# Sharing one weight stream between pairs of token tiles, and loading ahead across block boundaries

## Chip, cores and metric

The kernel runs on one core of a Trainium2 chip (trn2). The metric is the device time of one execution in microseconds. Engines are named as in the profile: PE (TensorE; PEld is its weight load), DVE (VectorE), ACT (ScalarE), POOL (GpSimd, which issues the gathers) and SP (SyncE, which issues most other transfers).

## What is computed

One layer of a decoder, in float32, for a prompt of 1024 tokens and for 8 sample tokens that each continue a cached sequence. Cut to what matters here:

```python
def layer(x, c, core, lw):
    sh1, sc1, gt1, sh2, sc2, gt2 = adaln(c, w_ada, b_ada)
    h = rmsnorm(x, g_norm1) * (1 + sc1) + sh1
    rq, rk, rv, rg, aq, ak, av = mixer_projections(h, w_in, g_qn, g_kn)   # w_in: 1024 x 3584
    o_ret, o_att, state = core(rq, rk, rv, aq, ak, av)                    # retention + dilated attention
    x = x + gt1 * mixer_output(o_ret, rg, o_att, g_ret, w_out)            # w_out: 1024 x 1024
    h2 = rmsnorm(x, g_norm2) * (1 + sc2) + sh2
    x = x + gt2 * peer(h2, w_pq, sub_keys, peer_u, peer_v)                # w_pq: 1024 x 1024
```

`peer` scores 2 x 128 keys per token and head, keeps 16 experts of 16384, and for each of the 8 x 16 chosen experts reads one row of `peer_u` and one of `peer_v` (8 KB together, stored side by side as `uv`): a dot product with h2, a GELU times a softmax gate, and a weighted sum of the `peer_v` rows.

## The kernel before, in words

`build` runs three blocks, one after the other. `condition` computes the six tables of the conditioning vectors from w_ada, in 12 chunks of 2 MB. `decode` handles the 8 sample tokens (w_in, w_out, w_pq in 11 chunks of 2 MB through three buffers, and the cache). `layer` handles the prompt in T = 8 tiles of 128 tokens, and takes nearly all of the time. Each block has its own SBUF tensors and starts its transfers when the block before has ended.

Within `layer` two kinds of work are interleaved by hand.

The **expert loop** runs over N = 64 pairs of tile and head, each with 16 experts per token. Experts go two at a time (GRP = 2), so there are 8 steps q per head, 64 steps g per tile, 512 in all. In a step POOL issues two gathers (line 857), each of 128 rows of 8 KB into one of 8 ring slots; DVE makes the two dot products (L1401) and, in between, one of eight parts of the choice of experts for the head after next (`choose_next`, from the scores `sc`); ACT computes GELU and gate and weights the two value rows (L969, L972, L976); PE adds them up by 16 transposes into `psA` (L1140) and frees the two slots, for which POOL waits.

The **front** of a tile is everything before its experts: norm of x, the seven projections by w_in in the order ORDER, q/k norms, retention and attention over 8 heads, w_out, the second norm, w_pq and the queries. Each engine has a generator `front()` of pieces; after every step, `Pace.upto(g)` runs the pieces whose mark `when(t, o)` is due. The offset o counts 0 to 59: norm and turn of x to 3, w_in chunks at 3 to 16, attention at 18 to 41, w_out at 43 to 46, second norm to 50, w_pq at 52 to 55, queries at 57 to 59. The front of tile t runs during the experts of tile t-1, beginning 16 steps (LEAD) before them; tile 0 has no experts to run beside, and tile 1's is squeezed to three quarters.

```python
return -1 if t == 0 else o * 3 // 4 if t == 1 else (t - 1) * STEPS - LEAD + o
```

SP issues, in one fixed order, weight chunks of 1024 KB ([128, 4, 512], 2 KB rows) through NB = 3 buffers `w` (L751): 14 of w_in, 4 of w_out, 4 of w_pq per tile. Chunk i waits until PE has used chunk i-3 (`s_pj`). Between chunks SP stores keys (L769) and values (L773), loads gate and shift rows into `rows4` (L761, L762), the residual and scale rows into `sp[0]` and `pt` (L764, L765), the next x (L756), and moves x_mid (L778, L783) and y (L788). PE multiplies a chunk by four 512-column products (L1000), each shown as two instructions.

At the first step of a tile DVE closes the tile before (L1411, L1418): it waits until all its transposes are done, and, because `yT` lies in the tile `qk`, until the next tile's q/k has been turned (`s_T`) and its keys are stored (`s_owk`); PE turns the sum back (L1134) and goes on when DVE has read it.

Of the kernel before, what the change touches and what calls it, by code (L numbers as in the profile page):

```python
# [15 lines left out]
P = 128  # L16
# [13 lines left out]
WBUF = 3  # L30
ORDER = (4, 5, 0, 1, 2, 3, 6)
# [21 lines left out]
def build(nc, a):  # L53

    with ExitStack() as whole:
# [15 lines left out]
        condition(nc, a, sem, psT, psO, ident, tabs, subk)  # L71
        decode(nc, a, sem, psA, psS, psT, psO, ident, tabs, subk, sc_s)
        layer(nc, a, sem, psA, psS, psT, psO, ident, tabs, subk, sc_s)


def condition(nc, a, sem, psT, psO, ident, tabs, subk):

    ps = [psT[:, 0:512], psT[:, 512:1024]]
    with ExitStack() as ctx:
# [21 lines left out]
        w_ada = a["w_ada"].rearrange("(k p) n -> p k n", p=P)  # L101
        assert ADA_CHUNKS % WBUF == 0
# [73 lines left out]
def decode(nc, a, sem, psA, psT2, psT, psO, ident, tabs, subk, sc_s):  # L176
# [8 lines left out]
    with ExitStack() as ctx:  # L185
# [3 lines left out]
        w = [sb(f"w{i}", [P, KT, 512]) for i in range(WBUF)]  # L189
        xs = sb("xs", [B, D])  # L190
        xns = sb("xns", [B, D])
        junk = sb("junk", [B, D])
        xms = sb("xms", [B, D])
        h2s = sb("h2s", [B, D])
        rows = sb("rows", [NC9, 3, D])
        gts = sb("gts", [B, D])
        h2sT = sb("h2sT", [P, KT, B])
        q_s = sb("q_s", [B, D])
        qT_s = sb("qT_s", [P, HP * (ROWS_S + B)])
        hTs = sb("hTs", [P, KT, B])  # L200
        mixs = sb("mixs", [B, D])
        mixTs = sb("mixTs", [P, KT, B])
# [26 lines left out]
        s_w = [sem(f"sample_weight{i}") for i in range(WBUF)]  # L229
# [14 lines left out]
        s_xs = sem("sample_x_loaded")  # L244
# [33 lines left out]
        def _(sp):  # L278
# [6 lines left out]
            sp.dma_start(xs[:], a["x_sample"]).then_inc(s_xs, 16)  # L285
            for c in range(LOADS):
# [16 lines left out]
                sp.dma_start(w[c % WBUF][:], src).then_inc(s_w[c % WBUF], 16)  # L303

# [251 lines left out]
def layer(nc, a, sem, psA, psS, psT, psO, ident, tabs, subk, sc_s):  # L556
# [5 lines left out]
    LEAD = 16  # L562
    ROWS_S = HP * B
    NB = 3
    CK = KT // 2
    NIN = NPROJ * 2
    NCH = NIN + 8
    VW = H * VA

    def when(t, o):  # L570

        return -1 if t == 0 else o * 3 // 4 if t == 1 else (t - 1) * STEPS - LEAD + o

# [10 lines left out]
    with ExitStack() as ctx:  # L584
# [3 lines left out]
        w = [sb(f"w{i}", [P, CK, 512]) for i in range(NB)]  # L588
# [14 lines left out]
        x = sb("x", [P, D])  # L603
# [3 lines left out]
        rqw, kw, rv, srg = (rows4[:, i, :] for i in range(4))  # L607
        gt1row = rows4[:, 0:2, :].rearrange("p a c -> p (a c)")
        b2row = rows4[:, 2:4, :].rearrange("p a c -> p (a c)")
        osb = rqw  # L610
# [946 lines left out]
```

## Time and profile before

| | before |
|---|---|
| median of 3 runs | 3594.51 us (3583.96 to 3602.37) |
| profiled execution | 3593.3 us, span 3591.5 us |
| busy share of the span | PE 71%, PEld 50%, DVE 63%, ACT 57%, POOL 33% |
| moved by DMA | 1373.20 MB, mean 382 GB/s |
| by the POOL queue (gathers) and the SP queue | 1083.68 MB and 287.23 MB |
| mean granted clock of PE | 0.827 |
| `condition` and `decode` | 0 to about 264 us |
| `layer`, tile 0's front | 264 to about 417 us, then the experts |

The busy shares are means over stages with different limits. PE's clock has two levels, 1.2 and 2.4 GHz; the granted clock of a stretch is the mean of their shares of 2.4. The DMA share of a stretch is the mean busy share of the core's 16 DMA engines; it can stand slightly over 1.

### The profile page before, as it was taken

To read this page: it belongs to the slowest core of one execution; us is meant where nothing else is said; L and a number is where in the kernel's file an instruction comes from. 1 tells how busy PE (TensorE), PEld (TensorE's weight loads), DVE (VectorE), ACT (ScalarE), POOL (GpSimd) and SP (SyncE) were. 2 spreads that over 40 slices of the span, in tenths; PEclk is the share of its full clock that TensorE was granted. 3 is DMA by queue.
4 is the path that set the end of the run, shared out by engine and by line. 5 is a ranking of instruction groups with operands and counts; after the bars stand their busy time and mean duration, and the time that the engine had idled before them with its cause. 6 is when DMAs were issued, how large, how long until landed. Compare 5 with 4: busy or idle time off the path is not lost.

```text
span 3591.5 us, 35730 instructions
## 1 busy us (share of the span) xinstructions
PE 2546.8 (71%) x12243; PEld 1797.8 (50%) x12243; DVE 2251.8 (63%) x5368; ACT 2046.4 (57%) x3415; POOL 1168.4 (33%) x1054
## 2 busy tenths in 40 slices
PE   8778577668666877667776777677876777655556
PEld 2224246445555456445654465555655466554544
DVE  0132457666776577666776487666866487776774
ACT  0101257565766567565866477565856476665664
POOL 0000123333333234333333233333434233443443
PEclk9888797889777978879787889788887988876777
DMA  8736699999999999999999999999999999999998
GB/s 294 262 136 233 224 378 405 410 416 390 418 415 414 408 388 420 415 406 394 409 412 417 410 366 414 414 411 401 409 416 411 381 398 399 415 421 415 416 413 323
DMA packets 293654, 1373.20 MB, mean 382 GB/s; under 512 B 35168, under 2 KB 35664, under 8 KB 160096
## 3 DMA queue, kind: packets, MB, share of 16 engines
q0 software_dynamic: 149072, 1083.68, 73.6%
q1 hardware_dynamic: 144400, 287.23, 21.7%
q8 instruction: 96, 1.57, 0.2%
q14 instruction: 86, 0.70, 0.0%
HBM read 1356.74 MB, written 14.09 MB: 382 GB/s over the span
## 4 chain that ended last, share of the span: by engine, by line
DMA 42%; PE 23%; ACT 12%; DVE 9%; POOL 4%; issue 3%; POOLq 0%; DVEq 0%; ACTq 0%
DMA pr_ring<-uv,pr_expert 23%; PE pairS L1000 12%; DMA pr_w<-w_in 12%; PE pairA L1140 9%; ACT pr_ring L976 6%; DVE pr_ring L1401 5%; POOL pr_ring L857 4%; DMA pr_w<-w_pq 3%; DMA pr_w<-w_out 3%; ACT pr_act_h L972 1%; ACT L969 1%; ACT L923 1%; ACT pr_act_h L969 1%; PE pairT L1006 1%; PE bank L1081 0%
## 5 line engine op out<-in xcount | busy, mean ns | idle before, releaser
L857 POOL DMA_INDIRECT pr_ring<-uv,pr_expert x1024 | 1146.5, 1120 | 2129.6 <-PE pairA L1140 1806.2
L1140 PE MATMUL pairA<-sb_ident,pr_ring 128*128 128x128 f32 x8192 | 1286.3, 324 | 733.7 <-ACT pr_ring L976 723.2
L1401 DVE CUSTOM_DVE_ANT_0 pr_ring<-pr_ring,pr_h 128x1024 f32<-128x1024 f32 x1024 | 1242.2, 1224 | 671.1 <-DMA pr_ring<-uv,pr_expert 658.9
L1140 PEld LDWEIGHTS pairA<-sb_ident,pr_ring 128*128 128x128 f32 x8192 | 1167.6, 170 | 918.8 <-ACT pr_ring L976 843.1
L976 ACT ACTIVATE pr_ring<-pr_ring,pr_act_h 128x1024 f32<-128x1024 f32 x1024 | 1120.2, 1141 | 16.7
L1000 PE MATMUL pairS<-pr_w,pr_hT 128*128 128x512 f32 x1152 | 594.5, 667 | 180.0 <-DMA pr_w<-w_in 139.9
L969 ACT ACTIVATE pr_act_h<-pr_dot 128x2 f32<-128x2 f32 x512 | 104.1, 203 | 960.1 <-DVE pr_dot L1401 958.6
L1000 PEld LDWEIGHTS pairS<-pr_w,pr_hT 128*128 128x128 f32 x1152 | 238.3, 216 | 455.1 <-issue 339.4
L972 ACT ACTIVATE pr_act_h<-pr_act_h,pr_gate_h 128x1 f32<-128x1 f32 x1024 | 245.8, 287 | 16.9
L969 ACT ACT_TABLE_LOAD x136 | 174.5, 1283 | 16.2 <-DVE pr_dot L1401 13.8
L1000 PE MATMUL pairS<-pr_w,pr_turned 128*128 128x512 f32 x256 | 132.6, 669 | 31.2 <-DMA pr_w<-w_out 29.0
L1000 PEld LDWEIGHTS pairS<-pr_w,pr_turned 128*128 128x128 f32 x256 | 52.9, 216 | 92.6 <-issue 58.3
L1066 PE MATMUL pairS<-pr_kTva,pr_turned 64*128 64x512 f32 (+3 forms) x192 | 90.1, 581 | 11.3 <-DVE pr_st L1230 11.3
L146 PE MATMUL pairT<-ad_w,ad_cT 128*9 128x512 f32 x192 | 85.9, 602 | 9.9 <-DMA ad_w<-w_ada 9.9
L1401 DVE DVE_READ_ACCUMULATOR2_ANT pr_dot<- 128x1 f32 x1024 | 83.8, 82 | 0.0
L956 ACT ACT_TABLE_LOAD x64 | 82.1, 1283 | 1.1
L1081 PE MATMUL bank<-pr_kTva,pr_pt 128*128 128x65 f32 x504 | 80.2, 316 | 0.5 <-DVE pr_pt L1238 0.5
L1081 PEld LDWEIGHTS bank<-pr_kTva,pr_pt 128*128 128x128 f32 x504 | 78.5, 238 | 3.7 <-DVE pr_pt L1238 1.9
L1336 DVE MAX8 pr_top<-pr_work 128x8 f32<-128x128 f32 (+2 forms) x195 | 65.8, 337 | 4.6
L1337 DVE FIND_INDEX8 pr_pos<-pr_top,pr_work 128x8 uint32<-128x128 f32 (+2 forms) x195 | 64.2, 329 | 0.0
L164 DVE TENSOR_TENSOR ad_mod<-bank,ad_badaT 128x432 f32<-128x432 f32 x1 | 0.6, 606 | 99.7 <-PE bank L135 99.7
L1006 PE MATMUL pairT<-sb_ident,pr_sp 128*128 128x128 f32 x352 | 58.8, 302 | 5.7 <-ACT pr_sp L923 5.0
(278 smaller groups left out, 1917.1 us busy)
## 6 DMA issues: line engine op xcount, KB each, us to landing
pr_w<-w_in SPq DMA_DIRECT2D x112, 1024.0 KB, 17.5
pr_w<-w_out SPq DMA_DIRECT2D x32, 1024.0 KB, 20.4
pr_w<-w_pq SPq DMA_DIRECT2D x32, 1024.0 KB, 23.6
ad_w<-w_ada SPq DMA_DIRECT2D x12, 2048.0 KB, 8.1
pr_ring<-uv,pr_expert POOLq DMA_INDIRECT x1024, 11.5
de_w<-w_in SPq DMA_DIRECT2D x7, 2048.0 KB, 11.3
pr_rows<-h SPq DMA_DIRECT2D x16, 512.0 KB, 30.7
de_kv<-k_sel SPq DMA_DIRECT2D x4, 1024.0 KB, 12.0
```

The costliest lines, as they stand in the source:

```text
L146: last = pe.matmul(ps[c % 2][0:NC9, :], cT[:, k, :], w[c % WBUF][:, k, :], start=(k == 0), stop=(k == KT - 1))
L857: pool.indirect_dma_start(ring[r][:], None, a["uv"], bass.IndirectOffsetOnAxis(ap=index, axis=0)).then_inc(s_g[r], 16)
L956: act.activation(gate_h[n % 2][:], delta[n % 2][:], ACT.Exp, accum_out=gsum[n % 2][:, 0:1]).then_inc(s_ge, 1)
L969: act.activation(act_h[:, c], dot[:, c], ACT.Gelu).then_inc(s_gelu, 1)
L972: last = act.activation(act_h[:, s:s + 1], act_h[:, s:s + 1], ACT.Identity, scale=gate_h[u][:, s:s + 1])
L976: last = act.activation(ring[s % RING][:, D:2 * D], ring[s % RING][:, D:2 * D], ACT.Identity, scale=act_h[:, s:s + 1])
L1000: last = pe.matmul(psS[:, at:at + 512], lhs[:, k, :], w[i % NB][:, j, :], start=(k == 0), stop=(k == KT - 1))
L1006: last = pe.transpose(psT[:, at + k * P:at + (k + 1) * P], src[:, k * P:(k + 1) * P], ident[:])
L1066: last = pe.matmul(psS[:, c], aqT[e, h // 2, :], kT[e, h // 2, c], start=True, stop=True)
L1081: last = pe.matmul(out, pt[:, k * P:(k + 1) * P], va[:, k, h * VA:(h + 1) * VA], start=(k == 0), stop=(k == t))
L1140: last = pe.matmul(psA[:, k * P:(k + 1) * P], ring[s % RING][:, D + k * P:D + (k + 1) * P], ident[:], start=(h == 0 and s == 0 and k % 4 = ...
L1401: last = dve.tensor_tensor_reduce(ring[r][:, 0:D], ring[r][:, 0:D], h2[t % 2][:], 1.0, 0.0, ALU.mult, ALU.add, dot[:, s:s + 1])
```

## The change

Tiles 0 and 1 keep a front of their own. Tiles 2+3, 4+5 and 6+7 form pairs: the first tile's front norms and turns both x, and every w_in chunk is multiplied with both before its buffer is freed. The second tile's products go to the PSUM bank `psO[1]`, from which ACT copies them into a new tile `raw` (v directly to `va`); its own front then starts with the q/k norms. Its h lies in `sp[0]`, its x in `pt`. It uses the gate and shift rows that the first tile loaded.

Chunks become 512 KB (CK = 2) in NB = 4 buffers, freed by a semaphore of their own (`s_wu`); a projection is reported (`s_pj`) once PE has waited for its own last product. Marks are laid out anew: a pair's products are spread over about 34 steps, one chunk each. `w`, `x` and decode's `w`, `xs` are allocated across blocks, so that condition's queue issues xs and the first three weight chunks of decode, and decode's queue x and the first four chunks of layer. To make room, some tensors share memory (`junk`, `q_s`, `xms` in decode; `hit` with `cand`; one score tile `sc` for two), and PE makes a head's scores one step earlier (q = 5).

```diff
-        w = [sb(f"w{i}", [P, CK, 512]) for i in range(NB)]
+        w, s_w, x, s_x = early
+        raw = sb("raw", [P, 6, HW])
-        sc = [sb(f"sc{u}", [P, 2 * NK]) for u in range(2)]
+        sc = sb("sc", [P, 2 * NK])
-        hit = sb("hit", [P, TOPK, TOPK])
+        hit = cand
...
@@ condition, SP, after its last chunk @@
+            wd, s_wd, xs, s_xs = sample
+            sp.dma_start(xs[:], a["x_sample"]).then_inc(s_xs, 16)
+            for c in range(WBUF):
+                sp.dma_start(wd[c][:], w_in[:, :, c * HW:(c + 1) * HW]).then_inc(s_wd[c], 16)
...
@@ decode, SP, after its last chunk @@
+            w_next, s_w_next, x_next, s_x_next = early
+            sp.dma_start(x_next[:], a["x_all"][0:P, :]).then_inc(s_x_next, 16)
+            for i in range(NB):
+                ks, at = slice(i * CK % KT, i * CK % KT + CK), ORDER[i * CK // KT] * HW
+                sp.dma_start(w_next[i][:], w_in[:, ks, at:at + HW]).then_inc(s_w_next[i], 16)
...
@@ layer, marks @@
+        if t == 0:
+            return -1
+        if t == 1:
+            return o * 40 // 60
+        if t == 2:
+            return 40 + o * 68 // 82
+        if t in FIRST:
+            return (t - 1) * STEPS - 36 + o * 80 // 82
+        return (t - 1) * STEPS - 20 + o
+
+    def mark_product(t, i, q):
+        return when(t, 5 + 5 * i + q if t in FIRST else 3 + 2 * i + q // 2)
...
+    def mark(t, o):
+        return when(t, o + (40 if t in FIRST else 6 if t in SECOND else 18))
...
@@ layer, SP @@
             def load_x(t):
-                if t >= 1:
-                    spq.wait_ge(s_T, 15 * (t - 1) + 13)
+                if t in SECOND:
+                    spq.wait_ge(s_h2, t - 1)
+                elif t >= 1:
+                    spq.wait_ge(s_T, 14 * (t - 1) + 12)
...
             def load_rows(t):
-                spq.wait_ge(s_gated, t + 1)
...
+                if own(t):
+                    spq.wait_ge(s_gated, t + 1)
...
             for t in range(T):
+                late = NIN if own(t) else 0
+                if own(t):
+                    chunks(t, NB, NB + 13)
+                    store_keys(t)
+                    chunks(t, NB + 13, NB + NIN)
+                    store_values(t)
+                    if t in FIRST:
+                        store_values(t + 1)
+                else:
+                    store_keys(t)
...
                 load_rows(t)
+                if t + 1 < T and own(t + 1):
                     load_x(t + 1)
+                chunks(t, late + NB, late + 8 + NB)
                 store_mid(t)
+                if t + 2 in SECOND:
+                    load_x(t + 2)
+                chunks(t, late + 8 + NB, late + 16 + NB)
...
@@ layer, ACT: the second tile's projection i @@
+                            act.wait_ge(s_pjB, NPROJ * p + i + 1)
...
+                                act.activation(raw[:, i, :], psO[1][:], ACT.Silu if i == 5 else ACT.Copy).then_inc(s_evB, 1)
...
@@ layer, ACT: scores @@
                 act.wait_ge(s_sc, n + 1)
-                if n >= 2:
-                    act.wait_ge(s_scu, n - 1)
+                if n >= 1:
+                    act.wait_ge(s_scu, n)
...
@@ layer, PE @@
+            def product(t, n, q, lhs, out):
+
+                i = CHUNK0[t] + 4 * n + q
                 pe.wait_ge(s_w[i % NB], 16 * (i // NB + 1))
...
+            def alone(t, n, q, lhs, bank):
+
+                last = product(t, n, q, lhs, psS[:, bank * 512:bank * 512 + 512])
+                last.then_inc(s_wu, 1)
+                if q == 3:
+                    pe.wait_ge(s_wu, CHUNK0[t] + 4 * n + 4)
+                    pe.sem_inc(s_pj, 1)
...
+                                if t in FIRST:
+                                    last = product(t, n, q, hT, psS[:, n % 2 * 512:n % 2 * 512 + 512])
+                                    if q == 3:
+                                        last.then_inc(s_pj, 1)
+                                    if q == 0 and NPROJ * FIRST[t] + n > 0:
+                                        pe.wait_ge(s_evB, NPROJ * FIRST[t] + n)
+                                    last = product(t, n, q, hTB, psO[1][:])
+                                    last.then_inc(s_wu, 1)
+                                    if q == 3:
+                                        pe.wait_ge(s_wu, CHUNK0[t] + 4 * n + 4)
+                                        pe.sem_inc(s_pjB, 1)
+                                else:
+                                    alone(t, n, q, hT, n % 2)
...
@@ layer, PE: a head's scores, AHEAD = 3 heads early @@
-                    if q == 6 and n + AHEAD < N:
+                    if q == 5 and n + AHEAD < N:
...
@@ layer, DVE: before x_mid is written to qk @@
+                            if t >= 1:
+                                dve.wait_ge(s_oxm, 16 * t)
...
@@ layer, DVE: first step of a tile @@
                         dve.wait_ge(s_free, n * GROUPS)
-                        if t + 1 < T:
-                            dve.wait_ge(s_T, 15 * (t + 1) + 2)
-                        dve.wait_ge(s_owk, 16 * min(t + 2, T))
-                        if t >= T - 1:
-                            dve.wait_ge(s_oxm, 16 * T)
+                        if t + 1 < T and own(t + 1):
+                            dve.wait_ge(s_T, 14 * (t + 1) + 1)
+                            dve.wait_ge(s_owk, 16 * (t + 2))
+                        else:
+                            dve.wait_ge(s_oxm, 16 * (t + 1))
```

## Rows read from the trace of the kernel before

**Rows 1.** The page: GB/s in 40 slices of the span, and the SP queue.

```profile
GB/s 294 262 136 233 224 378 405 410 416 390 418 415 414 408 388 420 415 406 394 409 412 417 410 366 414 414 411 401 409 416 411 381 398 399 415 421 415 416 413 323
...
q1 hardware_dynamic: 144400, 287.23, 21.7%
```

**Rows 2.** Stretches: length, busy us per engine, granted PE clock, DMA share, GB/s.

```profile
417.00:567.00 150.00, 103.31 (x480) 68.29 (x480) 93.66 (x239) 77.40 (x131) 43.69 (x42) 0.84 0.94 369
...
1350.00:1750.00 400.00, 287.95 (x1489) 218.87 (x1488) 275.73 (x661) 259.07 (x427) 146.86 (x130) 0.85 1.01 409
...
3140.00:3540.00 400.00, 230.23 (x1249) 204.64 (x1248) 278.68 (x670) 250.41 (x431) 175.22 (x153) 0.74 1.01 417
```

**Rows 3.** Waits: engine and line, whom it waited for, us in total, times, longest.

```profile
POOL pr_ring L857 <- PE pairA L1140: 1806.2, 466, 20.1
...
DVE pr_ring L1401 <- DMA pr_ring<-uv,pr_expert: 658.9, 519, 5.4
...
PE pairS L1000 <- DMA pr_w<-w_in: 139.9, 41, 6.7
```

**Rows 4.** DMA issues: queue, times, KB each, median us from issue to landing.

```profile
pr_w<-w_in SPq DMA_DIRECT2D x112, 1024.0 KB, 17.5
pr_w<-w_out SPq DMA_DIRECT2D x32, 1024.0 KB, 20.4
pr_w<-w_pq SPq DMA_DIRECT2D x32, 1024.0 KB, 23.6
...
pr_rows<-h SPq DMA_DIRECT2D x16, 512.0 KB, 30.7
```

**Rows 5.** PE in order of time, 2770 to 2850: start, us, line, count [idle before].

```profile
2775.82 1.91 PE L1140 MATMUL pairA<-sb_ident,pr_ring 128*128 128x128 f32 x16
2777.57 3.60 PE L1000 MATMUL pairS<-pr_w,pr_hT 128*128 128x512 f32 x8
2781.01 1.91 PE L1140 MATMUL pairA<-sb_ident,pr_ring 128*128 128x128 f32 x16
...
2798.76 5.29 PE L1000 MATMUL pairS<-pr_w,pr_hT 128*128 128x512 f32 x8 [6.68 <-DMA pr_w<-w_in]
```

**Rows 6.** Stretches, columns as in rows 2: six tile boundaries, one stretch of products.

```profile
846.90:886.00 39.10, 34.77 (x178) 22.67 (x176) 19.78 (x50) 21.79 (x36) 12.01 (x12) 0.97 0.98 378
1242.80:1282.00 39.20, 33.37 (x156) 21.06 (x155) 20.16 (x49) 21.45 (x35) 8.85 (x10) 0.92 0.92 359
1642.70:1682.00 39.30, 31.13 (x165) 20.57 (x163) 19.52 (x47) 21.09 (x36) 13.07 (x12) 0.96 0.97 376
2039.10:2092.00 52.90, 41.18 (x211) 27.89 (x210) 25.41 (x64) 25.31 (x41) 14.69 (x15) 0.90 0.84 328
2442.10:2487.00 44.90, 39.02 (x208) 26.34 (x207) 24.75 (x62) 25.32 (x41) 14.35 (x14) 0.95 1.00 385
2839.50:2887.00 47.50, 36.71 (x182) 24.41 (x181) 21.07 (x55) 23.16 (x40) 13.37 (x12) 0.89 0.84 324
...
2770.00:2840.00 70.00, 51.69 (x225) 31.13 (x224) 43.72 (x99) 35.78 (x62) 20.98 (x19) 0.93 1.02 406
```

**Rows 7.** DVE and PE at decode's start in order of time; the chain at layer's start.

```profile
103.96 1.21 DVE L469 CUSTOM_DVE_ANT_0 de_junk<-de_xs 8x1024 f32<-8x1024 f32 x1 [2.35 <-DMA de_xs<-x_sample]
...
110.47 1.86 PE L389 MATMUL pairT<-de_w,de_hTs 128*8 128x512 f32 x2 [2.85 <-DMA de_w<-w_in]
...
263.92 4.06 DMA pr_x<-x_all
```

**Rows 8.** SP's own waits; the instructions on pr_w and pr_rows (ns min/median/max).

```profile
SPq L751 <- PE pairS L1000: 1621.8, 149, 69.2
...
L751 SPq DMA_DIRECT2D pr_w<-w_in x112: 367/368/525, 264.3 to 2846.9; - x112
...
L906 ACT ACTIVATE pr_rows<-pairS x8: 597/600/605, 313.1 to 2841.7; 128x512 f32<-128x512 f32 x8
```

More of the change, by code:

```diff
@@ L70, in build, with condition @@
         sc_s = keep("sc_s", [HP * B, 2 * NK])
[L71 to L76, printed above, removed]
+        w = [keep(f"w{i}", [P, CK, 512]) for i in range(NB)]
+        x = keep("x", [P, D])
+        s_w = [sem(f"weights{i}") for i in range(NB)]
+        s_x = sem("x_loaded")
+        early = (w, s_w, x, s_x)
+        with ExitStack() as before:
+            wd = [before.enter_context(nc.sbuf_tensor(f"sb_wd{i}", [P, KT, 512], F32)) for i in range(WBUF)]
+            xs = before.enter_context(nc.sbuf_tensor("sb_xs", [B, D], F32))
+            s_wd = [sem(f"sample_weight{i}") for i in range(WBUF)]
+            s_xs = sem("sample_x_loaded")
+            sample = (wd, s_wd, xs, s_xs)
+            condition(nc, a, sem, psT, psO, ident, tabs, subk, sample)
+            decode(nc, a, sem, psA, psS, psT, psO, ident, tabs, subk, sc_s, sample, early)
+        layer(nc, a, sem, psA, psS, psT, psO, ident, tabs, subk, sc_s, early)
+def condition(nc, a, sem, psT, psO, ident, tabs, subk, sample):
     ps = [psT[:, 0:512], psT[:, 512:1024]]
@@ L283, in cache @@
                 sp.dma_start(kv[n % KVBUF][:], src).then_inc(s_kv[n % KVBUF], 16)
-            sp.dma_start(xs[:], a["x_sample"]).then_inc(s_xs, 16)
-            for c in range(LOADS):
+            for c in range(WBUF, LOADS):
                 if c == WBUF:
@@ L788, in store_y, with chunks @@
                 spq.dma_start(a["y_prompt"][t * P:(t + 1) * P, :], xmid[:]).then_inc(s_st, 16)
-            load_x(0)
-            for i in range(NB):
-                chunk(i)
+            def chunks(t, lo, hi):
+                for c in range(lo, hi):
+                    n = CHUNK0[t + 1] - CHUNK0[t]
+                    if c < n:
+                        chunk(t, c)
+                    elif t + 1 < T:
+                        chunk(t + 1, c - n)
             for tile, src in consts:
@@ L800, in _ @@
             for t in range(T):
-                first = t * NCH + NB
-                for c in range(first, first + 8):
-                    chunk(c)
-                store_keys(t)
-                for c in range(first + 8, t * NCH + NIN):
-                    chunk(c)
-                store_values(t)
+                late = NIN if own(t) else 0
+                if own(t):
+                    chunks(t, NB, NB + 13)
[6 more added lines that the diff above has]
+                    store_keys(t)
                 if t >= 2:
@@ L918, in front @@
-                    act.wait_ge(s_var, 4 * t + 3)
+                    if own(t):
+                        tiles = (t, t + 1) if t in FIRST else (t,)
+                        yield when(t, 0)
+                        for v in tiles:
+                            act.wait_ge(s_varx, v + 1)
+                            act.activation(stdx[v - t], varx[v - t], ACT.Sqrt).then_inc(s_stdx, 1)
+                        for v in tiles:
+                            yield when(t, 3 + 2 * (v - t))
+                            act.wait_ge(s_xT, v + 1)
+                            for k in range(KT):
+                                last = act.activation(hT_of(v)[:, k, :], psT[:, k * P:(k + 1) * P], ACT.Identity,
+                                                      scale=tabs[:, 0, k, B:B + 1], bias=tabs[:, 1, k, B:B + 1])
+                            last.then_inc(s_xTA, 1)
@@ L1038, in front @@
+                    yield mark(t, 0)
+                    if own(t):
+                        pe.wait_ge(s_evA, 3 * EV[t] + 3)
+                    else:
+                        pe.wait_ge(s_evB, NPROJ * (SECOND[t] + 1))
+                        pe.wait_ge(s_q, 2 * t)
+                    pe.wait_ge(s_TA, 5 * t + 2)
                     for par in range(2):
```

508 lines of the change are left out of this document (305 added, 203 removed).

## The prediction

> A **step** here is one pass of the expert loop: two gathers of 128 rows, two dot products, two weightings, sixteen transposes. There are 64 steps per token tile, 512 in all. Sums are made against the profiled execution, 3593.3 us with a span of 3591.5; the median of the runs shown is 3594.5, so the two can be used for each other.
>
> **What bounds the kernel now.** I began with the slices of the page [rows 1]. From the seventh slice to the last but one the core moves 366 to 421 GB/s, mostly 400 to 420, whatever the engines do. The stretches say the same with the DMA share beside it [rows 2]: 409 to 417 GB/s at a share of 1.01, both where weights flow and in the last 400 us, where only gathers are left. So the 16 DMA engines are full from about 567 us to 3540 us. Then the waits [rows 3]: POOL waits 1806 us for PE to give back a ring slot, which looks like a loop bound by its latency. But DVE waits 519 times for a gather to land, and the rate does not change between stretches with very different work on PE, DVE and ACT. A step with nothing but gathers moves 2 x 1024 KB = 2.097 MB, at 417 GB/s 5.03 us, and that is what the last stretch does (400 us, some 80 steps). The bytes set the pace there; a step with a weight chunk is longer by the chunk's bytes. Before 567 us the DMA is not full [rows 1, 2], and there latency and PE count.
>
> **Bytes removed.** (1) w_in is loaded 112 times 1024 KB [rows 4], 14 per tile. With tiles 2+3, 4+5 and 6+7 sharing one stream, 3 x 14 = 42 such loads go: 44.04 MB. (2) The second tile of a pair reuses the gate and shift rows still in rows4: 6 of the 16 loads of 512 KB go [rows 4], 3.15 MB. The price of a byte: the SP queue moved 287.23 MB in 21.7% of the 16 engines' span [rows 1], 779 us, so 368.5 GB/s while it holds the engines; the gather-only stretch runs at 417. The removed bytes belong to the SP queue, so I take 368.5: 119.5 us and 8.5 us. At 417 they would be 105.6 and 7.5. Sum: **-128 us** (bounds -113 and -128).
>
> **The paired stretch.** For 28 steps per pair PE does a half-size chunk for both tiles each step, four 512-column products, as many as it does now for one whole chunk of one tile. At the upper clock level (2.4 GHz) the sixteen transposes take 2777.57 - 2775.82 = 1.75 us and the four products 2781.01 - 2777.57 = 3.44 us [rows 5], 5.19 together. DMA brings 2.097 + 0.524 = 2.62 MB in such a step, 6.41 us at 409 GB/s. So DMA stays the longer one. Today the step needs 3.15 MB for the same PE work, and PE stands waiting up to 6.68 us for w_in [rows 5], 139.9 us in all [rows 3].
>
> **Chunk size and lead.** 3 buffers of 1024 KB become 4 of 512 KB: the lead falls from 3 to 2 MB, and 134 remaining whole loads become 268, 92 more issues than now. SP spends 1622 us waiting for PE at that line [rows 8], so the issues themselves are hidden; uncovered, at 0.368 us an issue [rows 8], they would cost 34 us. In paired steps a buffer has three steps, 19 us, to be refilled, where twice the size lands in 17.5 us [rows 4]: enough. In w_out and w_pq PE takes two half chunks a step, so the refill has some 10 us, against half of 20.4 and 23.6: a few us late per tile. What is queued behind is the next step's transposes and so POOL's gathers; the ring's four steps cover that much, as they cover PE's 6.68 us now. The load of the pair's second x waits on SP for h2 of the tile two before; behind it stand the last w_pq chunks, whose buffers are not free by then anyway. I take 0, upper bound +10.
>
> The Trainium skill, page "DMA: Bandwidth & Descriptors", section Bandwidth, speaks against this edit: it asks for transfers of at least 1 MiB and gives about 2.0 us fixed cost per DMA. Estimated from that page, 92 more DMAs paid one after another would be +184 us. The trace bears the serial payment out nowhere that the DMA share is 1.01, since another queue fills the engines meanwhile.
>
> **Tile boundaries.** At the first step of a tile DVE waits for the last transposes, for the next tile's turned q/k and its stored keys, and PE stands in a w_in product. Six such stretches run below 411 GB/s [rows 6]: 39.1 us at 378, 39.2 at 359, 39.3 at 376, 52.9 at 328, 44.9 at 385, 47.5 at 324, together 35 us of lost transfer time. After the change the next tile's q/k has been turned and stored some 15 steps earlier, or lies in other buffers, and the products wait less for weights; the drain of the ring stays. I take half, **-17 us** (bounds 0 and -35).
>
> **Early loads.** At decode's start DVE waits 2.35 us for x_sample and PE then 2.85 us for the first weights [rows 7]; both loads now run during the previous block, behind its last chunk, so they delay nothing. I take -4 of 5.2, since part of the first wait is the change of blocks. At layer's start the chain begins with 4.06 us for x [rows 7]: -4. Together **-8 us** (bounds 0 and -9).
>
> **What is added outside the full stretch.** In tile 0 each unpaired projection ends with PE waiting for its own last product: 11 times something between the modelled tail and a semaphore hop. No row shows this wait; the nearest is the 0.16 us by which four products end after the next work may start, 3.60 against 3.44 [rows 5], so 2 us below and 6 above, nothing negative as it only adds. I take +3.5. Tile 1's front is squeezed from 45 into 40 steps in the first stretch, 369 GB/s [rows 2], 15 us lost there; +4 (0 to 10).
>
> **Edits at nothing.** ACT's 21 copies of the second tile's projections, about 0.60 us each [rows 8], come in steps where ACT's four expert operations leave it idle; PE waits for each before the next projection, one step later. DVE loses two copies per pair for them. One score buffer for two: DVE reads it at q = 1 and 2, ACT overwrites at q = 7, 25 us later. The aliases of decode and of the candidate table are used in order by one engine. The new wait on the stored x_mid is 50 steps old when reached. POOL's queue has nothing moved. If the cover of all this went, it would be some 13 us on ACT.
>
> **Sum:** 3593.3 - 128 - 17 - 8 + 3.5 + 4 = 3448, forecast **3450 us**, faster by 4%. With the bounds 3420 to 3500.
>
> **Rivals.**
> *PE becomes the bound in the paired steps.* 5.19 us at the upper level is 5.19/g at a mean granted clock g, and passes 6.41 below g = 0.81. The stretch of products from 2770 to 2840 had 0.93 [rows 6], but after waits of several us the products run slower (5.29 us, [rows 5]) and the gather-only stretch, with less on PE, had 0.74 [rows 2]. At 0.74: 7.01 us, 0.60 over 84 steps, +50: 3500 us. Against it: PE would be busy four fifths of each paired step. Chance 0.07.
> *Slower: half chunks come too late.* Place: PE's wait on a weight buffer. If the lead of 2 MB never covers a landing, each of the 92 added loads costs what a 512 KB load takes beyond its transfer, 4.06 [rows 7] - 1.28 = 2.78 us: +256, 3706 us, 3% slower. It decides from 1.6 us per added load, when the gain of 143 is gone. For it: PE waits for weights now, and tile 0 has nothing else to fill the DMA. Against it: three buffers of lead in most steps, and the same 2 KB rows as before. Chance 0.03. By the Trainium skill's 2.0 us (the page and section named above) it would be 3450 + 184 = 3634 us; no run here shows that payment.
> *The bytes were hidden.* If latency of the ring set the step, removed weights would only leave DMA idle, and the early loads alone would count: 3585 us. For it, POOL's 1806 us; against it, the share of 1.01. Chance 0.02.
> That the stream is not really shared is excluded by the code: the second tile issues no w_in chunk.
>
> **How the numbers follow.** The forecast has 0.88 with 3420 to 3500 as its own range. The range given is 3412 to 3515: it takes in the bounds and the first rival, and leaves out the other two and some slack. A measurement can tell about 0.5% from no change, 18 us. Faster 0.95 (forecast and first rival), same 0.02, slower 0.03.
>
> **What would show it.** Right: DMA total near 1326 MB, w_in 140 loads of 512 KB, GB/s still above 400 after 560 us, PE's wait for w_in well under 139.9 us, the boundary stretches nearer 400. Wrong: paired steps of 7 us or more with the DMA share under 0.95 and PE full (first rival); PE's waits for w_in, w_out, w_pq grown and GB/s sagging (second); GB/s down by 3% everywhere at the same step time (third).

## The result, and the profile after

The changed kernel takes 3500.45 us (median of 4 runs, 3499.32 to 3510.21) against 3597.63 us for the kernel before (3583.96 to 3602.37): ratio 0.9742, 95% interval 0.9709 to 0.9775, so 93 us faster. The forecast was 3450 and the range 3412 to 3515: the direction and the range held, the gain came out about a third smaller than forecast. That the range held is partly luck: 3500.45 lies at the very end of the 3420 to 3500 that the prediction called its own, and what the range adds above that is no term of the sum. The profiled execution took 3499.32 us with a span of 3497.5, almost the median.

The page of the kernel after: GB/s in the 40 slices, the total, the two large queues, and the weight loads (times, KB each, median us from issue to landing).

```profile
GB/s 311 260 152 203 196 373 381 392 374 414 414 401 396 390 394 413 406 415 415 408 413 406 387 393 413 405 415 416 411 406 406 384 396 403 421 420 413 414 419 316
DMA packets 272759, 1326.03 MB, mean 379 GB/s; under 512 B 36544, under 2 KB 37040, under 8 KB 139200
...
q0 software_dynamic: 149072, 1083.68, 75.9%
q1 hardware_dynamic: 123504, 240.05, 19.0%
...
sb_w<-w_in SPq DMA_DIRECT2D x140, 512.0 KB, 10.8
sb_w<-w_out SPq DMA_DIRECT2D x64, 512.0 KB, 11.7
sb_w<-w_pq SPq DMA_DIRECT2D x64, 512.0 KB, 11.5
```

The bytes fell as worked out, by 47.2 MB. Most of the full stretch is still full, but slices six to nine stand at 373, 381, 392 and 374 GB/s, where [rows 1] had 378, 405, 410 and 416. Next the waits for weights and for gathers, columns as in [rows 3].

```profile
POOL pr_ring L936 <- PE pairA L1339: 1684.4, 459, 21.6
...
DVE pr_ring L1627 <- DMA pr_ring<-uv,pr_expert: 634.3, 514, 10.6
...
PE pairS L1138 <- DMA sb_w<-w_pq: 51.8, 22, 5.7
...
PE pairS L1138 <- DMA sb_w<-w_out: 49.6, 22, 5.0
...
PE pairS L1138 <- DMA sb_w<-w_in: 14.9, 9, 2.5
```

PE's wait for w_in went from 139.9 us [rows 3] to 14.9, but its waits for w_out and w_pq, 29.0 and 31.9 us before, grew to 49.6 and 51.8. The weights are late in another place. The two lines of the kernel before:

```profile
PE pairS L1000 <- DMA pr_w<-w_pq: 31.9, 7, 5.6
...
PE pairS L1000 <- DMA pr_w<-w_out: 29.0, 7, 6.5
```

Two stretches of products shared by a pair (columns as in [rows 2]) show full rate, at which a step's 2.62 MB take 6.3 us; PE is busy 82% of them at a granted clock of 0.94.

```profile
1480.00:1640.00 160.00, 131.27 (x610) 85.59 (x611) 103.63 (x246) 97.63 (x169) 56.31 (x53) 0.94 1.02 415
2240.00:2400.00 160.00, 130.45 (x609) 84.83 (x610) 104.31 (x246) 96.92 (x166) 58.92 (x52) 0.94 1.02 415
```

Six tile boundaries of the kernel after, each 40 us, answer to [rows 6]:

```profile
865.00:905.00 40.00, 33.65 (x155) 19.79 (x153) 25.59 (x61) 22.25 (x38) 16.32 (x13) 1.00 1.02 414
1252.00:1292.00 40.00, 26.47 (x160) 23.02 (x159) 33.40 (x84) 32.90 (x52) 15.10 (x14) 0.83 1.01 409
1638.00:1678.00 40.00, 34.47 (x194) 24.03 (x192) 28.23 (x67) 24.64 (x43) 14.72 (x14) 0.97 1.02 415
2009.00:2049.00 40.00, 29.80 (x166) 26.42 (x165) 31.95 (x78) 31.16 (x48) 14.11 (x12) 0.76 0.97 382
2400.00:2440.00 40.00, 33.78 (x188) 22.94 (x187) 27.46 (x64) 24.07 (x42) 14.79 (x14) 0.98 1.02 416
2771.00:2811.00 40.00, 30.83 (x219) 25.93 (x218) 33.86 (x78) 32.19 (x49) 13.82 (x15) 0.96 1.01 406
```

They ran at 324 to 385 GB/s and lost 35 us against 411; now one of six, at 382, loses 2.8 us and the others less than 1 us together. So these stretches gave about 31 us. But a new loss stands shortly before three of the boundaries, where the second tile of a pair begins its attention (columns as in [rows 2]):

```profile
1210.00:1240.00 30.00, 20.57 (x101) 17.04 (x102) 27.05 (x75) 29.04 (x45) 8.88 (x8) 0.68 0.89 341
1970.00:2000.00 30.00, 24.64 (x147) 21.52 (x147) 26.98 (x72) 29.43 (x41) 10.34 (x10) 0.80 0.87 329
2730.00:2760.00 30.00, 24.26 (x139) 20.69 (x140) 26.75 (x67) 29.22 (x42) 10.11 (x10) 0.78 0.89 332
```

Here no product waits for a weight; ACT is busy for 29 of 30 us, eight or nine times with a load of a function table of 1.28 us, and the transposes wait for it. The three lose 17 us against 411 GB/s, so what is left of the 31 is about 14. The corresponding stretches before the change (1200 to 1240, 1590 to 1630 and 1990 to 2030 us) moved 401 to 408 GB/s.

Where did the rest go? DVE adds a finished tile to `xmid` at the first step of the next, so the starts of that instruction cut the run into tiles. Kernel before (tiles 0 to 6) and kernel after (ns of one, then first and last start in us; the last tile has a line of its own):

```profile
L1418 DVE TENSOR_TENSOR pr_xmid<-pairA,pr_xmid x7: 1224/1225/1226, 869.8 to 3224.4; 128x1024 f32<-128x1024 f32 x7
...
L1644 DVE TENSOR_TENSOR pr_xmid<-pairA,pr_xmid x7: 1224/1225/1225, 876.4 to 3130.7; 128x1024 f32<-128x1024 f32 x7
L1664 DVE TENSOR_TENSOR pr_xmid<-pairA,pr_xmid x1: 1226/1226/1226, 3467.8 to 3467.8; 128x1024 f32<-128x1024 f32 x1
```

The first tile is finished at 876.4 us; before it was 869.8, although decode and layer now find their first loads in place. The six tiles after it take 3130.7 - 876.4 = 2254.3 us (2354.6 before), the last 337.1 (338.2). So the whole gain lies in tiles 1 to 6, and the part up to the end of tile 0's experts, in which the fronts of tiles 1 and 2 run, got no faster. (These are single executions; the run no_drain, with the same schedule, finishes tile 0 at 885.8 us.) Two stretches of it:

```profile
440.00:640.00 200.00, 151.08 (x734) 106.70 (x733) 130.58 (x334) 131.81 (x217) 63.60 (x58) 0.86 0.98 379
640.00:857.00 217.00, 167.26 (x744) 105.00 (x742) 135.36 (x318) 124.37 (x219) 75.54 (x64) 0.90 0.98 392
```

Before, they ran at 385 and (640 to 847 us) 412 GB/s.

Late weights are worth reading in order of time: PE in the first tile of the first pair, at its w_pq (start, us, instruction, idle before it and what ended that), POOL's next gather, and the stretch (columns as in [rows 2]).

```profile
1114.16 1.94 PE L1339 MATMUL pairA<-sb_ident,pr_ring 128*128 128x128 f32 x16
1118.24 3.64 PE L1138 MATMUL pairS<-sb_w,pr_hT 128*128 128x512 f32 x4 [2.14 <-DMA sb_w<-w_pq]
1124.25 3.06 PE L1138 MATMUL pairS<-sb_w,pr_hT 128*128 128x512 f32 x4 [2.37 <-DMA sb_w<-w_pq]
1130.27 6.16 PE L1138 MATMUL pairS<-sb_w,pr_hT 128*128 128x512 f32 x8 [2.96 <-DMA sb_w<-w_pq]
1136.58 3.69 PE L1339 MATMUL pairA<-sb_ident,pr_ring 128*128 128x128 f32 x32
...
1138.79 0.94 POOL L936 DMA_INDIRECT pr_ring<-uv,pr_expert  x1 [19.35 <-PE pairA L1339]
...
1118.00:1142.00 24.00, 18.28 (x66) 9.83 (x67) 11.09 (x32) 8.20 (x15) 3.73 (x5) 0.72 0.85 324
```

Four chunks stand in a row here, and their products wait 7.5 us in all. The transposes that free ring slots stand behind them and come in one lump of 32 at 1136; until then POOL waits 19.35 us and issues no gather. In these 24 us the DMA engines are busy only 0.85 of the time and the core moves 324 GB/s.

### The profile page after: what moved, and what is told of

Read it like the earlier page. It is cut to its first block, busy times and chain, and to the rows that moved or that the text cites. A ratio compares the mean times of both kernels' runs of the same rounds, so it can differ in the third digit from the quotient of the medians.

```text
span 3497.5 us, 35906 instructions
## 1 busy us (share of the span) xinstructions
PE 2510.3 (72%) x12243; PEld 1758.0 (50%) x12243; DVE 2250.2 (64%) x5362; ACT 2037.0 (58%) x3417; POOL 1193.1 (34%) x1054
## 3 DMA queue, kind: packets, MB, share of 16 engines
q0 software_dynamic: 149072, 1083.68, 75.9%
## 4 chain that ended last, share of the span: by engine, by line
DMA 35%; PE 23%; ACT 16%; DVE 11%; issue 3%; POOL 3%; POOLq 0%; DVEq 0%; PEldq 0%; ACTq 0%
DMA pr_ring<-uv,pr_expert 25%; PE pairA L1339 11%; PE pairS L1138 9%; ACT pr_ring L1114 8%; DVE pr_ring L1627 6%; DMA sb_w<-w_out 4%; DMA sb_w<-w_pq 4%; POOL pr_ring L936 3%; ACT pr_act_h L1110 2%; ACT L1107 2%; PE bank L1138 2%; DMA sb_w<-w_in 1%; ACT L1060 1%; ACT pr_act_h L1107 1%; ACT pr_sp L1060 1%
## 5 line engine op out<-in xcount | busy, mean ns | idle before, releaser
L936 POOL DMA_INDIRECT pr_ring<-uv,pr_expert x1024 | 1170.0, 1143 | 2011.8 <-PE pairA L1339 1684.4
L1339 PE MATMUL pairA<-sb_ident,pr_ring 128*128 128x128 f32 x8192 | 1267.7, 322 | 758.1 <-ACT pr_ring L1114 742.0
L1339 PEld LDWEIGHTS pairA<-sb_ident,pr_ring 128*128 128x128 f32 x8192 | 1142.6, 168 | 963.8 <-ACT pr_ring L1114 884.0
L1138 PE MATMUL pairS<-sb_w,pr_hT 128*128 128x512 f32 x816 | 416.4, 647 | 74.8 <-DMA sb_w<-w_pq 51.8
L1138 PEld LDWEIGHTS pairS<-sb_w,pr_hT 128*128 128x128 f32 x816 | 158.3, 208 | 247.4 <-issue 145.9
L1138 PE MATMUL pairS<-sb_w,pr_turned 128*128 128x512 f32 x256 | 140.0, 689 | 52.4 <-DMA sb_w<-w_out 49.6
L1138 PE MATMUL bank<-sb_w,pr_sp 128*128 128x512 f32 x336 | 157.9, 593 | 0.0
L1138 PEld LDWEIGHTS pairS<-sb_w,pr_turned 128*128 128x128 f32 x256 | 52.3, 219 | 118.8 <-DMA sb_w<-w_out 66.3
L1138 PEld LDWEIGHTS bank<-sb_w,pr_sp 128*128 128x128 f32 x336 | 64.0, 191 | 80.8 <-issue 80.8
L1544 DVE TENSOR_TENSOR pr_qk<-pairS,pr_rows 128x512 f32<-128x512 f32 x16 | 11.1, 691 | 85.5 <-PEq L1147 85.3
## 6 DMA issues: line engine op xcount, KB each, us to landing
sb_w<-w_in SPq DMA_DIRECT2D x140, 512.0 KB, 10.8
sb_w<-w_out SPq DMA_DIRECT2D x64, 512.0 KB, 11.7
```

The costliest lines, as they stand in the source:

```text
L936: pool.indirect_dma_start(ring[r][:], None, a["uv"], bass.IndirectOffsetOnAxis(ap=index, axis=0)).then_inc(s_g[r], 16)
L1138: last = pe.matmul(out, lhs[:, k, :], w[i % NB][:, j, :], start=(k == 0), stop=(k == KT - 1))
L1339: last = pe.matmul(psA[:, k * P:(k + 1) * P], ring[s % RING][:, D + k * P:D + (k + 1) * P], ident[:], start=(h == 0 and s == 0 and k % 4 = ...
```

## The experiments

Each kernel was timed in five rounds beside the kernel before, and kernels are compared by their ratio to it, known to some ±0.3%; 0.01 of ratio is 36 us, and a difference of two kernels is known to some ±14 us. Each trace is of one execution.

**Sharing alone: no_pairs.**

The marks of the tiles follow, since each tile now makes its own products.

```diff
-    PAIRS = ((2, 3), (4, 5), (6, 7))
+    PAIRS = ()
...
```

> No tile shares a stream: the list of pairs is empty, so all eight tiles load w_in and the gate and shift rows themselves; half-size chunks, their four buffers, the early loads, the single score buffer and tile 1's front stay as in the changed kernel. Theory A (a byte costs what a full DMA needs for it): the 47.17 MB come back at 412 GB/s, +114 us, so 3615 us, and the rest of the change is worth about 20 us to the bad against the kernel before (3597). Theory A' (a byte of this queue costs what I forecast, 368.5 GB/s): +128 us, 3628 us. Rival B (sharing has a cost of its own, the evictions of the second tile and the longer front): less comes back than the bytes, 3570 to 3600 us, and the rest of the change is about neutral. Window rates should stay near 410 GB/s in all.

3616.49 us, ratio 1.0063 (1.0036 to 1.009). From here to the changed kernel the ratio falls by 0.0321, 115 us: 47.2 MB at 410 GB/s. Rival B is out. The interval of the difference, 100 to 131 us, holds theory A and, near its end, theory A' too. The SP queue's own row speaks for the price of A':

```profile
q1 hardware_dynamic: 147216, 287.25, 22.0%
```

22.0% of 3601.4 us are 792 us, against 19.0% of 3497.5 = 665 after: 128 us less, 369 GB/s; the gathers' packets took some 15 us more meanwhile (73.3% of the span against 75.9%), so both queues together fell by 113. And the run shows that the rest of the change is worth about 23 us to the bad.

**The same with the old lead: no_pairs6.** NB = 6 for the layer (four early buffers and two of its own).

> The run no_pairs with six buffers of 512 KB in place of four: the lead is 3 MB again as before the change, in space that the pairs' rows had held; no other difference. Theory A (what the change costs beside its gain is the shorter lead): 15 to 30 us less than no_pairs, 3587 to 3601 us, near or below the kernel before. Rival H (it is tile 1's shorter front, the drains or the single score buffer): 3611 to 3620 us, as no_pairs.

3566.76 us, ratio 0.9923 (0.9904 to 0.9942): 50 us less than no_pairs for a lead of 3 MB in place of 2, far more than the 15 to 30 expected, and 28 us under the kernel before. Rival H is out. The wait for w_in in no_pairs:

```profile
PE pairS L1136 <- DMA sb_w<-w_in: 159.0, 73, 7.0
```

Its finished tiles, six of which lie between the two starts:

```profile
L1642 DVE TENSOR_TENSOR pr_xmid<-pairA,pr_xmid x7: 1224/1224/1225, 892.6 to 3236.6; 128x1024 f32<-128x1024 f32 x7
```

The same wait in no_pairs6, by the two kinds of buffer:

```profile
PE pairS L1141 <- DMA sb_w<-w_in: 69.3, 41, 4.0
...
PE pairS L1141 <- DMA pr_w<-w_in: 53.3, 27, 4.0
```

Its finished tiles:

```profile
L1647 DVE TENSOR_TENSOR pr_xmid<-pairA,pr_xmid x7: 1223/1224/1225, 870.2 to 3199.5; 128x1024 f32<-128x1024 f32 x7
```

The two profiled executions differ by 22.4 us already when tile 0 is finished, and by 37.1 when tile 6 is.

**Less lead in the changed kernel: nb3.** NB = 3.

> Three weight buffers of 512 KB in place of four, a lead of 1.5 MB in place of 2 MB, all else as in the changed kernel. Theory A (the shorter lead gives time back): PE's waits for weights grow by half or more and the time by 10 to 25 us, to 3510 to 3525. Rival C (the waits are covered, since a long step is made up by the shorter ones behind it): the waits grow as much, the time stays within 5 us of 3500, except for what tile 0's serial front loses (seen in the end of the first step).

3558.81 us, ratio 0.9899 (0.9871 to 0.9927): 56 us given back for half a megabyte, more than either theory said. The waits for w_out and w_pq grew by a quarter to two fifths and w_in's almost threefold:

```profile
PE pairS L1138 <- DMA sb_w<-w_out: 68.9, 24, 5.4
...
PE pairS L1138 <- DMA sb_w<-w_pq: 63.6, 23, 6.5
...
PE pairS L1138 <- DMA sb_w<-w_in: 41.5, 27, 6.6
```

The stretch in which tile 1's front runs drops to 334 GB/s at a DMA share of 0.88 (columns as in [rows 2]):

```profile
440.00:640.00 200.00, 135.43 (x596) 88.95 (x597) 109.36 (x275) 110.20 (x175) 46.55 (x44) 0.82 0.88 334
```

**More lead in the changed kernel: lead.** The 12 KB of `raw` serve as three more chunk buffers while no second tile's rows live in them.

```diff
+        w = w + [raw[:, 2 * u:2 * u + 2, :] for u in range(3)]
...
-                if i >= NB:
-                    spq.wait_ge(s_wu, i - NB + 1)
+                if PREV[i] >= 0:
+                    spq.wait_ge(s_wu, PREV[i] + 1)
+                if BUF[i] >= NB and t in SECOND:
+                    spq.wait_ge(s_gated, t + 1)
+                    spq.wait_ge(s_owk, 16 * t + 16)
```

BUF and PREV hold each chunk's buffer and that buffer's previous chunk.

> The changed kernel with three more chunk buffers where the second tile's rows are not alive: in tiles 0 and 1 up to the first four chunks of tile 2, and in each second tile from its gate on to the first four chunks of the next pair, so a lead of 3.5 MB there; the second tile's chunks five to seven are issued ahead of its row loads. Schedule, bytes and all else as in the changed kernel. Theory A: tiles 0 and 1 together fall from 820 us by 15 to 25 us, the end of the first step by 2 to 5 us, the second tiles' waits for w_out and w_pq vanish; 3472 to 3485 us. Rival C (a larger lead cannot help where the engines' 412 GB/s are used up anyway): within 5 us of 3500.

3474.16 us, ratio 0.9665 (0.9644 to 0.9686), 28 us under the changed kernel, as theory A said. Tile 0 is finished 19 us earlier, and the next six tiles take 2240.2 us in place of 2254.3. The second tiles no longer wait for w_out and w_pq. The first tiles of pairs, where the buffers are taken, still do: of the 36.4 us at w_pq, 23 are theirs; the other 13 lie in tile 1's front. The three stretches in which ACT is full are there too (1190 to 1220, 1950 to 1980, 2700 to 2730 us: 346, 322 and 330 GB/s), so this loss is not the lead's. Finished tiles in lead:

```profile
L1672 DVE TENSOR_TENSOR pr_xmid<-pairA,pr_xmid x7: 1225/1225/1226, 857.4 to 3097.6; 128x1024 f32<-128x1024 f32 x7
```

The two stretches of tile 0's experts:

```profile
440.00:640.00 200.00, 157.55 (x756) 110.39 (x757) 133.24 (x334) 132.63 (x219) 65.19 (x60) 0.85 1.01 395
640.00:857.00 217.00, 170.80 (x796) 110.96 (x795) 138.30 (x327) 131.50 (x232) 78.41 (x67) 0.91 1.00 403
```

**The same bytes in smaller loads: fine.** CK = 1, NB = 8: 256 KB chunks, the lead of 2 MB unchanged.

> Weight chunks of 256 KB in place of 512 KB, eight buffers in place of four: the same bytes, the same rows, the same lead of 2 MB, 268 more loads. Theory A (lead counts, not the number of loads): 3490 to 3503 us; PE's waits for w_out and w_pq are no longer, as a buffer comes free after half as much work. Rival G (each load costs something of its own): at 0.368 us of issue each +99 us, 3600 us, or any rise of more than 15 us. The Trainium skill, page DMA: Bandwidth & Descriptors, section Bandwidth, gives about 2.0 us fixed per DMA; paid one after another that would be +536 us by that page.

3504.3 us, ratio 0.9752 (0.9724 to 0.978): no difference to the changed kernel that can be told, for 268 more loads. The +99 us of rival G are not there. The Trainium skill gives about 2.0 us fixed per DMA (page DMA: Bandwidth & Descriptors, section Anatomy of one DMA — SWDGE (gpsimd) path, and for that path; the prediction and the expectation name the section Bandwidth, and these loads are issued by SP). Paid one after another that would have been +536 us, an estimate from that page; no run here shows that payment. Landing times hardly follow the size (median us at the end):

```profile
sb_w<-w_in SPq DMA_DIRECT2D x280, 256.0 KB, 9.8
sb_w<-w_out SPq DMA_DIRECT2D x128, 256.0 KB, 11.6
sb_w<-w_pq SPq DMA_DIRECT2D x128, 256.0 KB, 13.7
```

**One chunk a step: spread.** For w_out and w_pq of the first tiles and the last, and w_out of the second tiles, in place of two.

```diff
-        return when(t, 5 + 5 * i + q if t in FIRST else 3 + 2 * i + q // 2)
+        return when(t, 5 + 4 * i + q if t in FIRST else 3 + 2 * i + q // 2)
...
-                            yield mark(t, 25 + 2 * j + q // 2)
+                            yield mark_out(t, j, q)
```

> The products of w_out and w_pq of the first tile of each pair and of the last tile take one half-size chunk per step in place of two, those of w_out of the second tiles too; room for it comes from the empty step after each paired projection, which goes, and a start one step later. Same bytes, same buffers. Theory A (two chunks a step are more than the 2 MB lead and the queue's share can follow): PE's waits for w_out and w_pq (238 us with the weight loads) fall by half or more, the steps of 13 to 16 us in tiles 2 to 7 go to 7 or less, the time falls by 5 to 15 us to 3486 to 3495. Rival C (those waits are covered by the ring and cost nothing, since a long step is made up by shorter ones after it): waits fall as much but the time stays within 3 us of 3500.

3498.6 us, ratio 0.9739 (0.9716 to 0.9763): PE's waits for w_out and w_pq fell from 101 to 32 us, the time stayed, as rival C said. So most of the waits that PE shows at w_out and w_pq are not paid one for one. In the one execution traced, tiles 1 to 6 took 2241.3 us, 13 less, and tile 0 was finished 11 us later, at 887.6; single executions differ by about as much (no_drain: 885.8), so whether something was gained in one place and lost in the other stays open. The waits in spread (columns as in [rows 3]):

```profile
PE pairS L1147 <- DMA sb_w<-w_pq: 21.9, 9, 5.2
...
PE pairS L1147 <- DMA sb_w<-w_out: 10.1, 4, 3.6
```

**The drains: no_drain.** Readers wait for the count of used chunks.

```diff
                 last.then_inc(s_wu, 1)
-                if q == 3:
-                    pe.wait_ge(s_wu, CHUNK0[t] + 4 * n + 4)
-                    pe.sem_inc(s_pj, 1)
```

> PE no longer waits for its own last product of a projection and no longer signals it by an instruction of its own: whoever reads the projection waits for the count of used weight chunks, which the product's last matmul raises. All else as in the changed kernel. Theory A (late weights are what gives time back): 3497 to 3501 us, a gain of 0 to 3 us that lies in the serial front of tile 0. Rival C (the drains hold up DVE and ACT, 85 us and 75 us of waits put down to them): 3475 to 3485 us, and the steps of w_out and w_pq get shorter.

3506.01 us, ratio 0.9754 (0.973 to 0.9779): nothing gained, rival C is out. The trace says why. In the kernel after, DVE's wait at w_out stands at PE's sequencer, 85.3 us; without the drain the same wait (columns as in [rows 3]) stands at the product itself:

```profile
DVE pr_qk L1544 <- PE pairS L1144: 80.0, 9, 14.5
```

DVE waited for the products, and these in part for weights (w_out: 54.3 us in no_drain); the drain was only the last event before it went on.

**The early loads: no_early.** Both are moved back to the start of their own block.

> The early loads are undone: decode loads its own x_sample and first weights, the layer its own x and first four chunks, each at its own start as before the change. All else as in the changed kernel. Theory E (they are worth what I forecast): +8 us, 3508 us, and the first expert step ends near 441 us in place of 432.7. Rival F (tile 0's serial front gives it back, since its weights arrive no earlier behind the first four chunks): 3500 to 3504 us, the first step ends at 432 to 436 us.

3510.09 us, ratio 0.9767 (0.9736 to 0.9797). The times alone cannot tell 0 from 18 us, but the serial part can be read directly. The first dot product of the experts in order of time (start, us), in the kernel after:

```profile
430.29 1.23 DVE L1627 CUSTOM_DVE_ANT_0 pr_ring<-pr_ring,pr_h 128x1024 f32<-128x1024 f32 x1
```

And in no_early:

```profile
434.28 1.23 DVE L1622 CUSTOM_DVE_ANT_0 pr_ring<-pr_ring,pr_h 128x1024 f32<-128x1024 f32 x1
```

4.0 us between these two. But spread and squeeze45, whose code up to here is that of the changed kernel, have 426.54 and 429.88, so the early loads are worth 4 to 8 us: between half and all of what I forecast. Before the change it was 428.44, so tile 0's front itself got longer by about what the early loads gave. That follows the lead: with three buffers (nb3) the same point lies at 440.28, with seven (lead) at 426.72, with six (no_pairs6) at 424.78.

**Tile 1's front: squeeze45.** Tile 1 over 45 steps, tile 2 over the 62 behind it.

> Tile 1's work is laid over 45 steps as before the change in place of 40, and tile 2's over the 62 that follow in place of 67. Theory D (tile 1's squeezed front costs the time that tile 0's experts lost, 434.0 us against 416.1): 3490 to 3496 us, with the first 64 steps 5 to 10 us shorter. Theory A (the lead decides there too, at 2 to 3 chunks a step): 3497 to 3503 us, as tile 2 pays what tile 1 gets.

3507.81 us, ratio 0.9756 (0.9731 to 0.978): no gain; theory D in this form is out. Tile 0 was finished 3.6 us earlier, at 872.8, the six tiles after it took 2264.5 us, 10 more; neither is resolved.

**Steps given out by weights: smooth, smooth_lead, lead_even.** smooth is spread with tile 1's 40 steps laid out by weight demand (18 steps for the projections, 12 for its short attention, 13 for the rest) and tile 2 likewise; smooth_lead adds the buffers of lead; lead_even is lead with tile 1's layout alone:

```diff
-        if t == 1:
-            return o * 40 // 60
-        if t == 2:
-            return 40 + o * 68 // 82
+        if t == 1 and o < 18:
+            return o
+        if t == 1 and o < 41:
+            return 18 + (o - 18) * 12 // 23
+        if t == 1:
+            return 30 + (o - 41) * 13 // 18
+        if t == 2:
+            return 44 + o * 63 // 82
```

> The schedule of the run spread, and for tiles 1 and 2 the steps are given out by weight demand: tile 1's projections take 18 steps in place of 12, its attention over 256 keys 12 in place of 15, w_out and w_pq 13 in place of 12; tile 2 starts at step 44 and does one chunk a step for the paired projections, its attention in 14 steps. Same bytes and buffers. Theory D (the front of tiles 1 and 2, where the weights asked for come in lumps, is what lost 25 us more against 412 GB/s than before the change): tiles 0 and 1 together fall from 820 us to 795 to 805, total 3475 to 3488. Rival C (those lumps are made up by the short steps that follow, and the loss is latency of the attention steps): within 5 us of the run spread, 3494 to 3504.

3490.53 us, ratio 0.9722 (0.9692 to 0.9752): between the two theories and not resolved from either.

> Both the schedule of the run smooth and the three more buffers of the run lead. Theory A: the two mend the same waits from two sides, so less than the sum: 3466 to 3480 us, tiles 0 and 1 together 785 to 800 us. Rival C: as smooth, 3485 to 3495 us.

3469.9 us, ratio 0.9657 (0.9635 to 0.9678): the buffers decide, and what the layout adds to them (0.9665 without) is not resolved.

> The run lead, and tile 1's steps given out as in smooth (18 for the projections, 12 for its attention, 13 for the rest), with tile 2 starting at step 44 and laid evenly over the 63 that follow; the paired tiles are otherwise as in the changed kernel. Theory A with D (lead and the lumps of tile 1 are two separate losses, and smooth_lead lost again in tile 2 what it won in tile 1): tiles 0 and 1 together 785 to 798 us in place of 808, total 3455 to 3468. Rival (with the lead there the lumps no longer cost): 3468 to 3478, as lead.

3467.24 us, ratio 0.9647 (0.9626 to 0.9667): the fastest of all, 34 us under the changed kernel, though its step from lead is not resolved. Tile 0 is finished at 847.5 us, 29 earlier than in the changed kernel, and the second half of its experts sees the full rate. The six tiles after it take 2254.4 us, though, 14 more than in lead, so the 10 us won up to there are lost again in this execution (stretches, columns as in [rows 2]):

```profile
440.00:640.00 200.00, 154.80 (x759) 107.73 (x758) 130.89 (x326) 135.67 (x225) 65.19 (x62) 0.86 1.01 401
640.00:847.00 207.00, 167.05 (x780) 108.60 (x779) 136.58 (x320) 126.41 (x221) 75.38 (x65) 0.91 1.02 414
```

## Why the prediction was right, and where it was not

**What bounds the kernel: right.** Bytes paced it before and after. Removed bytes came off the time almost one for one, and the paired steps ran at the full rate of the DMA, 6.3 us by bytes where 6.41 was worked out, so the rival "PE becomes the bound" is out, although its 3500 us is the time that was measured: that is a coincidence. "The bytes were hidden" is out too.

**Bytes removed: right, the price not settled.** Forecast 128 us, shown 115, in an interval of 100 to 131. The price came from the whole SP queue, 368.5 GB/s. That queue's rows give 411 GB/s for what was removed when the kernel before is set against the changed one (779 us fell to 665), and 369 when no_pairs is (792 fell to 665). The second pair of kernels differs by the sharing and the marks that go with it alone, so I can't call 368.5 too dear.

**Paired stretch: right.** A buffer has time enough there; the wait for w_in is down to 14.9 us.

**Chunk size and lead: the step that failed.** The text says: "a few us late per tile. What is queued behind is the next step's transposes and so POOL's gathers; the ring's four steps cover that much", and takes 0 with an upper bound of +10.

The lateness was seen, its price was not: PE's waits at w_out and w_pq are 101 us over eight tiles, 61 before. Without pairs, 3 to 2 MB costs 50 us; with pairs, 2 to 1.5 MB costs 56, and three more buffers for part of the time give back 28. In w_out and w_pq PE takes two chunks a step, in one place four in a row, so four buffers are at most two steps, some 13 us (an estimate from the 6.41 us of a paired step), against 11.7 us to land: little is left. The ring does not cover it, because a late weight also holds back the transposes that free the ring: both streams stop, and the engines stand idle, as from 1118 to 1142 us (share 0.85, 324 GB/s). That the price of the lead is made up of such places is argued: the runs show the price, spread shows that most of PE's waits at w_out and w_pq could go without a gain that can be told, and in nb3 36 of the 66 us by which its traced execution is longer are there when tile 0 is finished (912.2 us), before any tile of a pair has its experts.

My error was to check the wait against the ring's depth instead of asking what the DMA engines would be moving during it. That the number of loads costs nothing was right as far as can be told: 268 more changed 4 us of 3500, within the noise. So the slower rival's price per added load is out; what it feared, weights that come late, did happen.

**Edits at nothing: a term is missing.** The prediction looked for ACT's added work at the copies of the second tile's projections and took 0. ACT is full elsewhere: in the three stretches where a second tile begins its attention, and there 17 us of transfer time are lost. The new marks have no term of this kind in the sum. What in them packs ACT so was not tried.

**Tile boundaries: right place.** Forecast -17 with a bound of -35; the six stretches show about -31, of which about 14 are left when the three stretches before them are counted in. That they reached the total is argued from the sum, since no run took the boundaries alone; no_pairs6, at 28 us under the kernel before with all of the change but the sharing and the short lead, agrees with a gain of this order.

**Early loads: half to all.** -8 forecast, 4 to 8 us in the traces.

**What is added.** The drains (+3.5 forecast) cannot be told from 0. Tile 1's shorter front (+4) is not resolved alone by squeeze45; lead_even finishes tile 0 a further 10 us earlier than lead and loses 14 in the tiles after it, so the layout of that front moves time about; that it gains any is not shown.

**The sum.** The terms of the prediction add to 3448, but its bounds add to 3423 and 3506, not to 3420 and 3500. Shown are, for everything but sharing and lead, -28 (no_pairs6), for the lead +50 (no_pairs against no_pairs6), and for the sharing -115, together -93. Term by term, -115 - 31 - 4 makes -150, so some 55 us are missing. 28 of them, with an uncertainty of 14, were won back by run lead; 17 stand where ACT is full. What is left is within the noise, and how it divides stays open; in the first tiles of pairs no space was left for more buffers, so that wasn't tried.

## What to carry to other kernels

When a loop is bound by transfers, price removed bytes at the rate of the full stretch and at that of their own queue, as bounds, and then ask of every edit that shrinks prefetch what each queue still has open while a consumer waits for the other; time in which both stand still is lost, since the bytes left are the same. Space spent on sharing a stream is taken from its lead: count how many steps the buffers last where chunks are used fastest, not where they are used on average. Tensors that live for part of a round can lend their space as buffers for the rest of it. And when work is moved to other steps, look for the stretch in which an engine that was never the bound, here ACT, is full.

## What was not expected of the hardware

Time from issue to landing of a weight load hardly depended on its size while the engines were full: w_in 10.8 us for 512 KB and 9.8 for 256 KB at the same 2 MB in flight, but 19.0 us for 512 KB with 3 MB in flight (no_pairs6). It goes with what is in flight rather than with its own size; that the loads ahead set it is argued, and 1.5 MB in flight (nb3) still took 10.4 us. And PE's granted clock in the paired stretch, 0.94, was higher than the 0.74 of the gather-only stretch [rows 2]: with more products PE ran nearer to the upper level (2.4 GHz), not farther.
